# One step of a hybrid decoder on one core: the inverse of two prompt chunks' triangles, packed in one 128x128 matrix and multiplied in whole-array products

## The reference, cut to what matters

```
kk    = k @ k.T
a_mat = I + where(strictly lower, beta * decay * kk, 0)        # C x C
sol   = triangular_solve(a_mat, [beta*v, beta*exp(gamma)*k])   # needs inv(a_mat)
w = u - wk @ s ; o = qg @ s + qk @ w ; s = g_last * s + kd.T @ w
```

## Time and profile before

| | us |
|---|---|
| median of three runs (2064.64 to 2065.83) | 2065.24 |
| the profiled execution | 2066.47 |
| its span | 2064.7 |
| PE busy | 2049.2 (99%) |
| DVE busy | 1202.4 (58%) |
| ACT busy | 769.7 (37%) |
| POOL busy | 193.9 (9%) |

### The profile page before, as it was taken

The page is one execution under the profiler, slowest core; times in us unless marked ns, Lnnn a source line. Parts: engine busy times, 40 slices in busy tenths (PEclk is TensorE's granted clock), DMA queues, the critical chain, the costliest instruction groups (busy, mean ns, idle before and its releaser), DMA issues.

```text
span 2064.7 us, 35229 instructions
## 1 busy us (share of the span) xinstructions
PE 2049.2 (99%) x15045; PEld 2012.7 (97%) x15045; DVE 1202.4 (58%) x2063; ACT 769.7 (37%) x926; POOL 193.9 (9%) x352
## 2 busy tenths in 40 slices
PE   9999999999999999999999999999999999999997
PEld 9999999999999999999999999999999999999997
DVE  7989787666676666645454544444444444444444
ACT  6434554223333333333343433333242333333343
POOL 7322011111231110000000000000000000000001
PEclk9999999999999999999999999999999999999999
DMA  7554454454555444654444545444444444444443
GB/s 249 146 147 142 145 173 139 149 156 148 174 152 152 148 144 125 193 185 148 153 148 148 152 147 152 152 146 152 151 147 152 153 145 152 152 146 153 149 148 111
DMA packets 297114, 316.07 MB, mean 153 GB/s; under 512 B 9928, under 2 KB 290672, under 8 KB 296704
## 3 DMA queue, kind: packets, MB, share of 16 engines
q1 hardware_dynamic: 291616, 291.54, 46.2%
q0 software_dynamic: 5056, 22.16, 3.5%
q10 hardware_dynamic: 288, 0.15, 0.0%
HBM read 305.38 MB, written 8.42 MB: 152 GB/s over the span
## 4 chain that ended last, share of the span: by engine, by line
PE 98%; DVE 1%; DMA 1%; ACT 0%; issue 0%; DVEq 0%; POOL 0%; POOLq 0%
PE main L1608 31%; PE main L1610 30%; PE main L1609 30%; PE aux L1759 3%; PE main L1648 1%; PE aux L1866 0%; PE aux L1737 0%; PE aux L1688 0%; DMA raw<-in_w_back 0%; DMA raw<-in_w_in 0%; PE aux L1805 0%; DVE merged L938 0%; PE aux L1721 0%; PE aux L1772 0%; PE aux L1773 0%; DVE lo L938 0%
## 5 line engine op out<-in xcount | busy, mean ns | idle before, releaser
L938 DVE TENSOR_TENSOR lo<-raw,hi 128x1024 fp32r<-128x1024 f32 x544 | 658.5, 1225 | 351.2 <-ACT hi L659 344.0
L659 ACT ACTIVATE hi<-raw 128x1024 fp32r<-128x1024 f32 x544 | 566.9, 1055 | 688.0 <-DMA raw<-in_w_up 223.7
L1608 PE MATMUL main<-x_hi,hi 128*128 128x320 f32 x2624 | 820.6, 313 | 1.3 <-DVE scratch L938 1.3
L1610 PE MATMUL main<-x_hi,lo 128*128 128x320 f32 x2624 | 810.8, 309 | 0.0
L1609 PE MATMUL main<-x_lo,hi 128*128 128x320 f32 x2624 | 810.7, 309 | 0.0
L1608 PEld LDWEIGHTS main<-x_hi,hi 128*128 128x128 f32 x2624 | 492.6, 188 | 12.2 <-issue 9.6
L1609 PEld LDWEIGHTS main<-x_lo,hi 128*128 128x128 f32 x2624 | 492.7, 188 | 0.7
L1610 PEld LDWEIGHTS main<-x_hi,lo 128*128 128x128 f32 x2624 | 492.5, 188 | 0.0
L1608 PE MATMUL main<-o_hi,hi 128*128 128x320 f32 x1408 | 441.5, 314 | 0.0
L1610 PE MATMUL main<-o_hi,lo 128*128 128x320 f32 x1408 | 435.0, 309 | 0.0
L1609 PE MATMUL main<-o_lo,hi 128*128 128x320 f32 x1408 | 435.0, 309 | 0.0
(11 more groups left out here) (276 smaller groups left out, 1226.8 us busy)
## 6 DMA issues: line engine op xcount, KB each, us to landing
raw<-in_w_in SPq DMA_DIRECT2D x210, 512.0 KB, 3.6
raw<-in_w_up SPq DMA_DIRECT2D x128, 512.0 KB, 3.7
raw<-in_w_down SPq DMA_DIRECT2D x128, 512.0 KB, 3.5
raw<-in_w_back SPq DMA_DIRECT2D x80, 512.0 KB, 3.5
head_rows<-row_scratch POOLq DMA_DIRECT2D x8, 640.0 KB, 6.1
scratch<-in_s_in POOLq DMA_DIRECT2D x8, 512.0 KB, 4.8
out_s_out<-scratch POOLq DMA_DIRECT2D x8, 512.0 KB, 4.5
merged<-in_x SPq DMA_DIRECT2D x8, 320.0 KB, 7.6
```

Of the source, the lines that this page charges most:

```text
L659: act.activation(HI[:, slot * TILE:(slot + 1) * TILE], RAW[:, slot * TILE:(slot + 1) * TILE], ACT.Copy).then_inc(hi_ready, 1)
L938: return dve.tensor_tensor(out, a, b, op)
L1608: pe.matmul(bank, hi, xh, start=first, stop=False)
L1610: return pe.matmul(bank, lo, xh, start=False, stop=last)
```

## The change

Two chunks in one matrix. The second chunk's triangle is no longer transposed as the first is: its product is made with swapped operands, and its decay with the opposite sign (`LD1`), so it lies in the upper triangle, and the two are added in one 128x128 matrix `LP`. The diagonal 32x32 blocks go to `LP32`, the rest to `LP4` and `LP5` (made by POOL). The samples have their own 64-column matrix `LS`.

The levels on PE. Instead of 32x32 tile products, levels 0 to 3 have one product with a 128x128 stationary matrix (`LP32`, or `BTF`, the small blocks spread over the diagonal) and 32 moving columns; in levels 0 and 1 a second one for the samples with a 64-column stationary matrix (`LS`, `YYS`) and 64 columns. Level 4 is one product of 32 columns in each step; level 5 one of 64 columns in the odd step and two in the even one (stationary of 64 columns with 128 moving, then 128 with 64). Placement and the order of steps stay.

On DVE step 1 has 14 instructions before `x_ready` in place of 10, and one (`spread`) before the two of QKD; even steps 4 to 10 get a product with a triangle mask ahead of `x_ready` and a `spread` behind it; steps 11 to 14 are small copies and scalings. Step 0 has one more. On ACT step 0 has one more exponential. POOL gets two instructions in the decay part, `LP4` and `LP5` after `lp_ready`, and the placing of the blocks in XT after `xq_done`, and loses the two clearings between heads. Its masks are built between the first strips of the q, k, v phase instead of at the start.

```diff
+fm = FM.rearrange("p (m j c) -> p m j c", m=6, j=4)
+near = QKV[:, 18 * N + 6 * P:18 * N + 6 * P + 6 * CB]
+
+def same_block(i):
+    s, m = 2 << i, FM[:, i * P:(i + 1) * P]
+    select(m, [[-s, P // s], [0, s]], 0, 1)
+    select(m, [[s, P // s], [0, s]], s - 1, -1)
...
+def triangles():
+    lower, upper = near[:, 5 * CB:6 * CB], TRI[:, 6 * CB:7 * CB]
+    for i in range(4):
+        halves = lambda t: t.rearrange("p (q t x) -> p q t x", t=2, x=2 << i)
+        for t, tri in ((0, lower), (1, upper)):
+            ins = pool.tensor_tensor(halves(TRI[:, i * CB:(i + 1) * CB])[:, :, t, :],
+                                     halves(near[:, i * CB:(i + 1) * CB])[:, :, t, :], halves(tri)[:, :, t, :],
+                                     ALU.mult)
+    ch.link(ins)
+    for i in range(4):
+        r = slice(CB * i, CB * (i + 1))
+        ch.link(pool.tensor_copy(TRI[r, 4 * CB:5 * CB], (lower, upper)[i % 2][r, :]))
+        ch.link(pool.tensor_copy(TRI[r, 5 * CB:6 * CB], (lower, upper)[i // 2][r, :]))

...
-level_mask(0)
...
-level_mask(1)
...
-for level in range(2, 6):
-    level_mask(level)
-select(FM[:, 0:P], [[-2, P // 2], [0, 2]], 0, 1)
...
-with pool.Fori(1, 12) as s:
+for s, build_masks in ((1, lambda: (same_block(0), same_block(1))), (2, lambda: (same_block(2), same_block(3))),
+                       (3, lambda: (same_block(4), same_block(5))), (4, far_masks), (5, near_masks), (6, triangles)):
+    build_masks()
+    history(s, s, s * 2, s * 2 + (2 + BANKS))
+with pool.Fori(7, 12) as s:
     history(s, s, s * 2, s * 2 + (2 + BANKS))
...
     pool.wait_ge(dt_exp, h + 1)
-    pool.tensor_tensor(DTM, DTM, MASKI[:], ALU.mult).then_inc(dtm_ready, 1)
+    pool.tensor_tensor(DTM, DTM, MASKI[:], ALU.mult)
+    ch.link(pool.tensor_scalar(LP32, MASKI[:, 0:P], -1.0, 1.0, ALU.mult, ALU.add))
+    pool.tensor_tensor(LD1, LD1, LP32, ALU.mult).then_inc(dtm_ready, 1)
     if h % 4:
         pool.wait_ge(ss_stored, h * 32)
...
                        ALU.mult).then_inc(qg_ready, 1)
     if h + 1 < HEADS:
         head_rows_in(h + 1)
+    pool.wait_ge(lp_ready, h + 1)
+    pool.tensor_tensor(LP4, LP, FAR[:, 0:P], ALU.mult)
+    pool.tensor_tensor(LP5, LP, FAR[:, P:2 * P], ALU.mult).then_inc(lp_far, 1)
+    pool.wait_ge(xq_done, h + 1)
+    ch.link(pool.tensor_tensor(UPQ.rearrange("p (u c) -> p u c", u=2), XQ.rearrange("p (u c) -> p u c", u=2),
+                               TRI[:, None, 6 * CB:7 * CB].to_broadcast([P, 2, CB]), ALU.mult))
+    for u in range(2):
+        ins = pool.tensor_tensor(XT[:, u * P:(u + 1) * P].rearrange("p (j c) -> p j c", j=4),
+                                 UPQ[:, None, u * CB:(u + 1) * CB].to_broadcast([P, 4, CB]),
+                                 OWN[:, 0:4, None].to_broadcast([P, 4, CB]), ALU.mult)
+    ins.then_inc(xt_placed, 1)
     pool.wait_ge(dn_done, h + 1)
     pool.dma_start(A["s_out"][:, h].rearrange("b k v -> k b v"),
                    SS.rearrange("p (b v) -> p b v", b=DB)).then_inc(ss_stored, 16)
     pool.dma_start(A["p_out"][h], S1).then_inc(ss_stored, 16)
-    if following:
-        pool.memset(XT[:, 0:NP], 0.0)
-        pool.memset(XX[:, 0:NP], 0.0).then_inc(x_cleared, 1)

...
     if k == 0:
         act.wait_ge(dt_ready, h + 1)
-        act.activation(DTM, DTM, ACT.Exp).then_inc(dt_exp, 1)
+        act.activation(DTM, DTM, ACT.Exp)
+        act.activation(LD1, LD1, ACT.Exp, scale=-1.0).then_inc(dt_exp, 1)
         act.wait_ge(rows_loaded, 16 * (h + 1))
...
+def two(t):
+    return t.rearrange("p (u c) -> p u c", u=2)
+
+def spread(out, t, n, at):
+
+    return tt(out.rearrange("p (j c) -> p j c", j=n), t[:, None, :].to_broadcast([P, n, CB]),
+              OWN[:, at:at + n, None].to_broadcast([P, n, CB]), ALU.mult)
...
@@ -1300,6 +1342,7 @@

             ins = ts(DTM[0:n, lo:hi], BG_[0:n, lo:hi], cols(COL, h, 1, c * 56 + 8, 1, n),
                      ALU.subtract, 0.0, ALU.min)
+        ins = ts(LD1, BG_[:, P:2 * P], cols(COL, h, 1, 56 + 8, 1), ALU.subtract, 0.0, ALU.max)
         ins.then_inc(dt_ready, 1)
...
     elif k == 1:
         dve.wait_ge(tok_psum, h + 1)
         dve.wait_ge(dtm_ready, h + 1)
-        tt(LT[:, 0:NP], AX[0][:, 0:NP], DTM[:, 0:NP], ALU.mult)
-        link(tt(LT[0:NS, NP:N], AX[1][0:NS, N:N + NS], DTM[0:NS, NP:N], ALU.mult))
-        for i in range(4):
-            ins = tt(blocks(YYC, i), diagonal(LT, i), mask(0, i), ALU.mult)
-        link(ins)
-        tt(XTC[:, 0:2 * CB].rearrange("p (u c) -> p u c", u=2), mask(5),
-           YYC[:, 0:2 * CB].rearrange("p (u c) -> p u c", u=2), ALU.subtract)
-        link(tt(XTC[0:NS, 2 * CB:3 * CB], CM[0:NS, 5 * CB:6 * CB], YYC[0:NS, 2 * CB:3 * CB], ALU.subtract))
-        dve.transpose(XXC[:, 0:2 * CB], XTC[:, 0:2 * CB])
-        dve.transpose(XXC[0:NS, 2 * CB:3 * CB], XTC[0:NS, 2 * CB:3 * CB]).then_inc(x_ready, 1)
+        tt(LP, AX[0][:, 0:P], DTM[:, 0:P], ALU.mult)
+        link(tt(LP32, AX[0][:, P:2 * P], LD1, ALU.mult))
+        link(tt(LP, LP, LP32, ALU.add))
+        dve.sem_inc(lp_ready, 1)
+        tt(LS[0:NS, :], AX[1][0:NS, N:N + NS], DTM[0:NS, NP:N], ALU.mult)
+        link(tt(LP32.rearrange("p (j c) -> p j c", j=4), LP.rearrange("p (j c) -> p j c", j=4),
+                OWN[:, 0:4, None].to_broadcast([P, 4, CB]), ALU.mult))
+        tt(two(YYS[0:NS, :]), two(LS[0:NS, :]), pairs(0, NS), ALU.mult)
+        link(tt(YP, LP32[:, 0:2 * CB], LP32[:, 2 * CB:4 * CB], ALU.add))
+        tt(XT[0:NS, NP:N], ident[0:NS, 0:NS], YYS[0:NS, :], ALU.subtract)
+        link(tt(PAIR[:, 0:CB], YP[:, 0:CB], YP[:, CB:2 * CB], ALU.add))
+        link(tt(PAIR[:, CB:2 * CB], PAIR[:, 0:CB], PAIRS[:, 0:CB], ALU.mult))
+        link(tt(XTQ, UNIT[:], PAIR[:, CB:2 * CB], ALU.subtract))
+        dve.transpose(XXS[0:NS, :], XT[0:NS, NP:N])
+        link(dve.transpose(XXQ, XTQ))
+        link(tt(two(PAIR), two(XQ), triangle(0), ALU.mult))
+        dve.sem_inc(x_ready, 1)
+        spread(BTF, PAIR[:, 0:CB], 4, 0)
         for n, c in both:
             tt(QKD[0:n, c], AX[1][0:n, c], DTM[0:n, c], ALU.mult)
     elif k < 15 and k % 2:
         level = (k - 3) // 2
         dve.wait_ge(y_psum, h * 6 + (level + 1))
         if level < SMALL_LEVELS:
-            ins = tt(YYC[:, 0:2 * CB].rearrange("p (u c) -> p u c", u=2),
-                     AX[0][:, 0:2 * CB].rearrange("p (u c) -> p u c", u=2), mask(level + 1), ALU.mult)
+            ins = tt(YP[:, 0:CB], AX[0][:, 0:CB], PAIRS[:, (level + 1) * CB:(level + 2) * CB], ALU.mult)
             if level < 2:
-                ins = tt(YYC[0:NS, 2 * CB:3 * CB], AX[0][0:NS, 2 * CB:3 * CB],
-                         CM[0:NS, (level + 1) * CB:(level + 2) * CB], ALU.mult)
-        else:
-            m = LM[:, (level - SMALL_LEVELS) * P:(level - SMALL_LEVELS + 1) * P]
-            ins = tt(YY[:, 0:NP].rearrange("p (c i) -> p c i", c=2),
-                     AX[1][:, 0:NP].rearrange("p (c i) -> p c i", c=2),
-                     m[:, None, :].to_broadcast([P, 2, P]), ALU.mult)
-        ins.then_inc(y_ready, 1)
+                ins = tt(two(YYS[0:NS, :]), two(AX[0][0:NS, CB:CB + NS]), pairs(level + 1, NS), ALU.mult)
...
+        n = CB << (level - SMALL_LEVELS)
+        dve.tensor_copy(YP[:, 0:n], AX[1][:, 0:n]).then_inc(y_ready, 1)
+        if level == 5:
+            dve.wait_ge(xt_placed, h + 1)
+            for i in (0, 2):
+                at, own, other = CB * (i + 1), slice(CB * i, CB * (i + 1)), slice(CB * (i + 1), CB * (i + 2))
+                dve.transpose(XT[own, at:at + CB], PAIR[other, 0:CB])
+                dve.tensor_copy(XT[own, P + at:P + at + CB], PAIR[own, 0:CB])
     elif k < 15:
         level = (k - 4) // 2
         dve.wait_ge(z_psum, h * 6 + (level + 1))
-        if level < SMALL_LEVELS - 1:
-            ins = tt(XTC[:, 0:2 * CB], XTC[:, 0:2 * CB], AX[0][:, P:P + 2 * CB], ALU.subtract)
-            c = slice(2 * CB, 3 * CB)
+        if level < SMALL_LEVELS:
...
+                ins = tt(XT[0:NS, NP:N], XT[0:NS, NP:N], AX[0][0:NS, P + CB:P + CB + NS], ALU.subtract)
+            link(ins)
+            ins = dve.transpose(XTQ, XXQ)
             if level == 0:
...
+                ins = dve.transpose(XXS[0:NS, :], XT[0:NS, NP:N])
             link(ins)
-            ins = dve.transpose(XXC[:, 0:2 * CB], XTC[:, 0:2 * CB])
-            if level == 0:
-                ins = dve.transpose(XXC[0:NS, c], XTC[0:NS, c])
-            ins.then_inc(x_ready, 1)
-        elif level == SMALL_LEVELS - 1:
-            link(tt(XTC[:, 0:2 * CB], XTC[:, 0:2 * CB], AX[0][:, P:P + 2 * CB], ALU.subtract))
-            for i in range(4):
-                ins = dve.transpose(diagonal(XX, i, 2), XTC[CB * i:CB * (i + 1), 0:2 * CB]
-                                    .rearrange("p (u c) -> p u c", u=2))
-            ins.then_inc(x_ready, 1)
-            for i in range(4):
-                dve.tensor_copy(diagonal(XT, i, 2), XTC[CB * i:CB * (i + 1), 0:2 * CB]
-                                .rearrange("p (u c) -> p u c", u=2))
+            link(tt(two(PAIR), two(XQ), triangle(level + 1), ALU.mult))
```

(58 more changed lines are left out.)

87 lines of the change are left out of this document (45 added, 42 removed).

## The result

The changed kernel takes 2077.99 us (median of 4 runs, 2077.45 to 2078.33), the one before 2065.53 beside it; the ratio is 1.006, its 95% interval 1.0043 to 1.0078. The forecast was 2063.8 and its range ended at 2069.5: it was wrong on the side of rival C, and by more than that rival's 2072. The profiled execution took 2077.45 us, its span is 2075.7, 11.0 above the span before. The rise is 0.6%, small, but well outside the interval.

What follows compares the result with a forecast made beforehand. PE was taken to bound the kernel, busy 2049.2 of 2064.7 us. The terms -7.1 + 3.75 + 0.9 + 0.7 + 0.3 gave -1.4 us, a median of 2063.8, with an 8-in-10 range of 2058.8 to 2069.5.

Steps and rivals of the forecast that it cites:

- rival C: DVE's step 1: POOL's two products hold it 0.96 us, state products pushed in; +3 to +7 us, 2068 to 2072; chance 0.22.
- PE's price, eight heads: PE's steps in the heads: cost without waits falls 0.9 us per head, 7.1 us over eight.
- waits at step 4, six later heads: PE waits for step 3's masking on DVE: 0.4 us in four heads, 1.3 in one, 0.85 in one; 3.75 us.
- waits in the other steps 3 to 14: Heads 0 and 4: 0.9 us at head 0's step 3, 0.7 swallowed by its existing wait, 0.3 in head 4.
- PE's part: PE's step prices after: one narrow product 0.22 us, a mixed step 0.60, level 5's even step 0.79.
- Rival B: PE's narrow products cost by their columns, 0.05 us instead of 0.22: 2056 us, or 2051 with the 64-column form free; chance 0.06.
- The cover: Free time between step 3's masking on DVE and PE's step 4: 1.0 us in head 2, 0.1 in head 1.
- DVE's part: DVE from step 1 to step 3's masking: 0.8 us longer, 0.2 for the spread, 0.45 for meeting POOL; masking 1.45 later.
- every further microsecond is one on PE: At step 3's masking on DVE: once the cover ends, each further microsecond of lateness is one on PE.
- PE's stream there does not wait for them: nothing: Masks built by POOL between strips of the q, k, v phase: no cost on PE, at most 0.2 us gained.
- The last line of the prediction: Signs of being wrong: narrow products below 0.1 us, step 1's small DVE products taking twice their time, PE waiting in q, k, v.

Runs made afterwards that it cites:

- dummy products: Kernel before the change with four more linked 128-column DVE products, read by nobody, in step 1: 2070.45 us, ratio 1.0024.
- the run with POOL's products later: Changed kernel with POOL's two far-block products held until step 3's masking is done: 2073.37 us (one run).
- all six held: Changed kernel with POOL's four state products and two far-block products held until step 3's masking is done: 2068.97 us (one run).
- later places: Changed kernel with steps 4 to 7 of the six later heads placed 2, 2, 2 and 1 blocks further down PE's stream: 2072.32 us, ratio 1.0026.
- early masks alone: Changed kernel with the masks' block selects back at the start and their products between strips 1 to 3 instead of 4 to 6: 2081.29 us (one run).
- the wide matrices: Changed kernel with the 64-column stationary matrices of levels 0, 1 and 5 read 128 columns wide: 2072.25 us (one run).
- DVE's order: Changed kernel with QKD behind step 3's masking in every head, and the gate's two products too in the six later heads: 2069.61 us, ratio 1.002.
- the last kernel: Changed kernel with all edits that helped, and POOL's state products held until step 3's masking as well: 2057.54 us, 0.9958 of the kernel before.

## Why the prediction was wrong

In spans: forecast -1.4 us, measured +11.0. By the terms of the sum, for the two profiled executions:

```
                                         forecast   measured
PE's price, eight heads                    -7.1       -7.1
waits at step 4, six later heads           +3.75      +8.0
waits in the other steps 3 to 14           +1.9       +5.7
steps 1 and others                          0         +0.4
half clock, on main products                0         +2.2
q, k, v phase, at 145 us                    0         +1.3
start and end of the program                0         +0.5
```

1. PE's part was right in each piece: 0.22, 0.60 and 0.79 against 0.22, 0.59 and 0.79. (Its own terms give 8 x (5.64 - 4.73) = 7.3; that 7.1 was met to the tenth is luck.) Rival B fell. The Trainium skill, TensorEngine Tiling (Array Packing), section Performance Considerations, would make two records of 32 columns 0.05 us, an estimate from its 60 cycles; the trace has 0.22 and does not agree.

2. The cover was right: 1.0 and 0.1 forecast, 0.9 and 0.1 by the dummy products in heads 2 and 1.

3. The step that failed is "DVE's part", the lateness of step 3's masking, taken as 1.45 us in every head; measured are 1.7 in heads 1, 2, 3 and 7, 2.1 in head 6 and 2.8 in head 5. In head 2 I had 1.45 us: 0.8 for step 1 itself, 0.45 for POOL's two products, 0.2 for the spread. Measured are 0.93 (3.20 - 2.27, in the run with POOL's products later), 0.34, and 0.46 between `x_ready` and the masking, of which the separate semaphore instruction is 0.12: 1.73. Against a cover of 0.9 a miss of 0.3 turns a wait of 0.4 into one of 0.9. That "every further microsecond is one on PE" stands in the prediction; how near the estimate lay to the cover should have widened the range.

4. In head 1 the miss is the same 0.3 as in head 2, and not POOL's state products: the old step 1 there had met them too (3.13 us against 2.27 in head 2; now 4.31 against 3.54), and the cover of 0.1 was read with that in it. In heads 5 and 6 POOL was priced as in head 2, and there it failed: 0.85 and 0.4 forecast, 2.26 and 1.29 measured. In head 5 it is the greater length of step 1 alone that puts all four state products beside it. They start 2.3 us behind step 1 before and after, because POOL waits for a transfer ahead of them. The 0.8 us in the decay part, which rival C had as the cause, move nothing there, and the dummy products in the kernel before bring out the same meeting. What the state products cost the changed kernel is 0.86 and 1.2 us at step 4 of heads 1 and 5 (1.41 and 1.76 with the far blocks held, both 0.55 with all six held). Head 6's extra 0.4 went with the two far-block products alone.

The Trainium skill, SBUF — State Buffer, section Who interferes with whom, calls the port pair that DVE and POOL share an exclusive lock, the other engine being fully blocked. Head 5 agrees: DVE's product of 32 columns takes 1.01 us and ends at 667.50, 0.05 behind the last of POOL's four, which ends at 667.45. In head 1 POOL's four last 1.5 us and DVE's step grows by 1.1 (4.31 - 3.20), because single products of DVE get through between two of POOL's (they end at 380.04, 380.29 and 380.79, POOL's at 379.96, 380.23 and 380.66).

5. In heads 0 and 4 step 3 comes so soon that it waits for step 1 with no queue between: 2.0 and 1.5 where I had 0.9 and, with its own wait taking it in, 0.3. Here rival C had the mechanism: POOL waits for no transfer, its decay part got 1.6 us longer and not 0.8, and the first state product, which started 0.44 and 1.28 us ahead of DVE's step 1, starts 0.84 and 0.58 behind it. With all six products held the waits are 0.95 and 0.53. The old waits at steps 10 and 6 did shrink (0.4 left, and none), but new ones came at steps 5, 10 and 14, probably since narrow products bring PE back sooner; no run tried that.

6. Nowhere did I price the clock. Behind two waits of 1.8 and 2.3 us came half clock for some 3 us each, and the end of the program ran at 0.50 where it had 0.82: six products there take 1.54 us in place of 0.88. The end may be chance: the clock falls there in all 17 kernels, between 2.5 and 5.6 us behind the last main product.

7. "PE's stream there does not wait for them: nothing" was wrong for the masks: four DVE products went from 1.28 to 2.47 us at 91 us, DVE was 2.0 behind and stayed so until PE needed it. I looked at whether POOL had time, not at what its products do to a DVE that has no slack. The last line of the prediction named this, and priced it at nothing.

Rival C named side and place, and the six waits at step 4 are in its range (8.0 of 7 to 11), but partly by luck: it had POOL's two products cost 0.96 us, and they cost 0.34; the rest is DVE's own work, 0.93 and 0.46, and the state products. Its chance of 0.22 was too low, its price too: it left out the clock and the q, k, v phase.

## What to carry to other kernels

Where a step's cover is known to 0.1 us, price what comes before it by what the engine does beside its neighbours there, in every head and not in the one that is quietest, and move queued work (here the gate and QKD, 1.3 us; moving them took 9.0 us off the heads, 3.4 of it by the clock) behind the urgent instruction before moving or cutting anything. A product with 64 stationary columns between whole-array ones is cheaper read 128 wide. Ask too what a longer step will run on beside: head 5 lost most by that. And where a wait of PE of 2 us is likely, count the clock with it: here it cost 1.7 us more each time it came, and it did not come each time.

## What the runs showed of the hardware

A float32 product with 128x128 stationary and 32 moving columns costs PE 0.22 us in the stream, as much as one with 128. Beside whole-array products a stationary matrix of 64 columns costs 0.15 us more than one read 128 wide in a mixed step (0.595 to 0.446), and 0.34 in level 5's (0.784 to 0.446). A separate semaphore instruction on DVE takes 0.12 us (gap 0.15 to 0.03). A DVE product of 32 columns takes 0.19 us alone and 0.32 to 1.01 beside POOL's.

The clock, over all traces: in the later heads it fell to half behind each wait at step 4 of 1.76 us and more (1.76, 1.78, 1.94, 2.25, 2.26, 2.32, 2.57, 2.59, 2.61), for about 3 us with 1.7 lost, and not behind those of 1.41 and less. At step 3 of head 0 a wait of 2.0 us brought half clock in two kernels (later places, early masks alone) and not in three others (the changed one, the wide matrices, DVE's order). At step 6 of head 4 it fell behind 1.85 in the last kernel. At 145 us it fell behind waits of 1.34, 1.35, 1.37, 1.41 and 1.41, and not behind 1.24, 1.25, 1.32, 1.38 and 1.40. So the length of the wait does not decide alone. What else does was not tried.
